# A fused decoder layer: the delta-rule chain of each head squeezed into an earlier part of its projection, and the output projection's operand loaded one unit sooner

## The reference, cut to what matters

```
h = rmsnorm(x, norm1_w[l])
mix, c, sg, sh = token_mixer(h, ...)          # proj = h @ w_in; both head groups; mix @ w_out
x = x + mix
u = jax.nn.relu(rmsnorm(x, norm2_w[l]) @ w_up[l])
x = x + (u * u) @ w_down[l]
```

## Time and profile before

| | before |
|---|---|
| median of 3 runs | 3074.03 us |
| the three runs | 3075.28, 3073.93, 3074.03 us |
| time of the profiled execution | 3074.89 us |
| its span, first to last instruction | 3073.1 us |
| mean granted TensorE clock | 0.986 |
| TensorE busy | 2974.0 us (97%) |
| VectorE busy | 2032.5 us (66%) |
| ScalarE busy | 1202.3 us (39%) |
| share of TensorE in the chain of work that ended last | 86% |

### The profile page before, as it was taken

One profiled execution on the slowest core, in us unless ns is written; L12 is line 12 of the kernel. 1 busy time (PEld: TensorE's weight loads), 2 busy tenths in 40 slices (PEclk: granted clock), 3 DMA queues, 4 the chain that ended last, 5 costly groups with the idle time before them and its releaser, 6 DMA issues.

```text
span 3073.1 us, 52508 instructions
## 1 busy us (share of the span) xinstructions
PE 2974.0 (97%) x22024; PEld 2918.8 (95%) x22024; DVE 2032.5 (66%) x2828; ACT 1202.3 (39%) x1522; POOL 316.9 (10%) x433
## 2 busy tenths in 40 slices
PE   7999999999999999979999999999998999999998
PEld 7999999999999999969999999999998999999998
DVE  5556463637464646545558777777778887878886
ACT  4333333323333333333334444444445444444454
POOL 5010101011101010110210000000000000000021
PEclk9999999999999999989999999999999999999999
DMA  7233563533232334343425444454448666666665
GB/s 211 56 82 64 74 67 53 84 59 83 60 75 61 82 61 82 67 128 104 121 82 153 145 145 156 138 163 136 158 141 276 194 193 196 197 192 192 195 194 192
DMA packets 514107, 392.61 MB, mean 128 GB/s; under 512 B 16752, under 2 KB 483904, under 8 KB 513872
## 3 DMA queue, kind: packets, MB, share of 16 engines
q1 hardware_dynamic: 462272, 268.86, 35.8%
q0 software_dynamic: 22832, 88.39, 7.9%
q10 hardware_dynamic: 28768, 32.00, 3.6%
HBM read 304.87 MB, written 84.33 MB: 127 GB/s over the span
## 4 chain that ended last, share of the span: by engine, by line
PE 86%; DVE 8%; ACT 3%; issue 2%; DMA 1%; POOL 0%; DVEq 0%; ACTq 0%; POOLq 0%
PE main L1267 38%; PE main L918 27%; PE mx L1267 6%; PE mx L1163 2%; PE mx L1062 1%; PE mx L1070 1%; PE mx L994 1%; PE mx L978 1%; DVE w_lo L1803 1%; DVE tmp L1911 1%; PE mx L1021 1%; PE mx L1029 1%; PE mx L1104 1%; PE mx L1170 0%; PE mx L1098 0%
## 5 line engine op out<-in xcount | busy, mean ns | idle before, releaser
L918 PE MATMUL main<-h_hi,w_hi 128*128 128x296 f32 (+1 forms) x2592 | 617.0, 320 | 21.8 <-DVE h_lo L2204 13.8
L1267 PE MATMUL main<-forms_a,w_hi 128*128 128x288 f32 x3072 | 617.9, 296 | 8.5 <-DVE forms_a L2390 4.6
L1267 PE MATMUL main<-forms_b,w_hi 128*128 128x288 f32 x3072 | 613.9, 295 | 7.2 <-DVE forms_b L2390 4.9
L918 PE MATMUL main<-h_lo,w_hi 128*128 128x296 f32 (+1 forms) x2592 | 570.3, 302 | 0.0
L918 PE MATMUL main<-h_hi,w_lo 128*128 128x296 f32 (+1 forms) x2592 | 568.9, 301 | 0.0
L1267 PEld LDWEIGHTS main<-forms_a,w_hi 128*128 128x128 f32 x3072 | 496.9, 189 | 9.6 <-issue 9.4
L1267 PEld LDWEIGHTS main<-forms_b,w_hi 128*128 128x128 f32 x3072 | 492.1, 188 | 8.5 <-issue 5.5
L1267 PE MATMUL main<-forms_a,w_lo 128*128 128x288 f32 x1536 | 456.3, 297 | 0.0
L918 PEld LDWEIGHTS main<-h_hi,w_hi 128*128 128x128 f32 x2592 | 420.5, 193 | 34.5 <-DVE h_lo L2204 15.4
L1267 PE MATMUL main<-forms_b,w_lo 128*128 128x288 f32 x1536 | 452.2, 294 | 0.0
L918 PEld LDWEIGHTS main<-h_lo,w_hi 128*128 128x128 f32 x2592 | 427.9, 192 | 0.0
(11 more groups left out here) (383 smaller groups left out, 3668.7 us busy)
## 6 DMA issues: line engine op xcount, KB each, us to landing
w_raw<-in_w_in SPq DMA_DIRECT2D x130, 512.0 KB, 8.2
w_raw<-in_w_up SPq DMA_DIRECT2D x128, 512.0 KB, 4.1
w_raw<-in_w_down SPq DMA_DIRECT2D x100, 512.0 KB, 4.4
u_forms<-ub POOLq DMA_DIRECT2D x32, 1152.0 KB, 6.7
z<-x_scratch SPq DMA_DIRECT2D x32, 576.0 KB, 7.0
x_scratch<-z POOLq DMA_DIRECT2D x31, 576.0 KB, 3.1
stage<-u_forms ACTq DMA_DIRECT2D x30, 576.0 KB, 4.1
w_raw<-in_w_out SPq DMA_DIRECT2D x32, 512.0 KB, 4.0
```

The source lines that it names most:

```text
L918: ins = mm(out[:, half, :], w[:, ring, k, :], x[:, kx, half * width:half * width + width], start=first and n == 0, stop=last_ and n == 2)
L1267: ins = mm(out, w[:, k, :], x[:, kx, :], start=i in (0, 1, 3) and k == 0 and n == 0, stop=k == KP - 1 and n == 2, skip_group_check=True)
```

## The change

Four tables and a few lines are changed.

1. The GDN chain from `t1` to `st_4` is spread over positions 25 to 57 instead of 25 to 63, so 32 stages take 32 steps rather than 38.
2. `out` of a GDN head is done in the same head, at position 61, and no longer as the stage `gdn_out` at position 2 of the next. `gates`, `conv_in` and `gates_b` of the HGRN2 part move from 3, 6 and 9 to 0, 5 and 8. ScalarE may do the first exponential of `gates` before the last main tile is evacuated.
3. In the last head SyncE issues the loads of k-tiles 0 to 6 of the output projection's operand when the last unit begins (`OUT_U0 - 1`), and no longer when it ends. ScalarE and VectorE split k-tiles 0, 1 and 2 ahead of the last head's GDN `out`.
4. The order of the first k-tiles becomes 0, 1, 2, 3, 7, 4, 5, 6; TensorE does three of them ahead of `turn_v`, and the counts in `FILL_TO` up to `out` are higher. The other splits, and the evacuations and weight splits of the output projection (`EARLY_AT`), are assigned to other stages.

The core of the diff (the two functions `split_hi` and `split_lo` are also moved up, unchanged):

```diff
-K_ORDER = [7] + list(range(7)) + list(range(8, KT))
+K_ORDER = [0, 1, 2, 3, 7, 4, 5, 6] + list(range(8, KT))
...
-SPLITS = {"gdn_out": (0,), "gates": (1,), "gates_b": (2,), "turn_k": (3,), "stw": (4, 5), "diag": (6,), "l1": (7,), "l4": (8,),
-          "l8": (9,), "l16": (10,), "l32": (11,), "l64": (12,), "o": (13, 14), "out": (15,)}
+LATE_SPLITS = {"l2": (8,), "l4": (9,), "l8": (10,), "l16": (11,), "l32": (12,), "l64": (13,), "o": (14,), "out": (15,)}
+SPLITS_HI = {"gates": (3, 4), "gates_b": (5, 6), "turn_v": (7,), **LATE_SPLITS}
+SPLITS_LO = {"gates": (3,), "gates_b": (5,), "turn_v": (6,), "turn_k": (7,), **LATE_SPLITS}
 EARLY = 8
-EARLY_AT = {"l2": 0, "l4": 1, "l16": 2, "l64": 3, "o": 4, "out": 5}
-FILL_TO = {"turn_v": 3, "turn_k": 4, "diag": 7, "l1": 12, "l2": 17, "l4": 22, "l8": 26, "l16": 30, "l32": 34, "l64": 39, "o": 45,
-           "out": 54, "st0": 71}
+EARLY_AT = {"l1": 0, "l2": 1, "l8": 2, "l32": 3, "o": 4, "out": 5}
+FILL_TO = {"gates": 3, "turn_v": 5, "turn_k": 6, "diag": 12, "l1": 16, "l2": 21, "l4": 26, "l8": 30, "l16": 34, "l32": 38, "l64": 43,
+           "o": 49, "out": 58, "st0": 71}
...
-                       + [f"{s}_{c}" for c in range(1, NW) for s in ("ws", "vn", "st")], 25, 63)}
-HG_STAGES = {"gdn_out": 2, "gates": 3, "conv_in": 6, "gates_b": 9, "turn_v": 10, "turn_k": 18, "stw": 20, "diag": 22,
+                       + [f"{s}_{c}" for c in range(1, NW) for s in ("ws", "vn", "st")], 25, 57),
+              "out": 61}
+HG_STAGES = {"gates": 0, "conv_in": 5, "gates_b": 8, "turn_v": 10, "turn_k": 18, "stw": 20, "diag": 22,
...
-            sp.wait_ge(s_unit, OUT_U0)
+            sp.wait_ge(s_unit, OUT_U0 - 1)
             sp.wait_ge(s_gmix, 16 * (HEADS - 1))
-            sp.wait_ge(s_hmix, 16 * (HEADS - 1))
...
+            sp.wait_ge(s_unit, OUT_U0)
+            sp.wait_ge(s_hmix, 16 * (HEADS - 1))
             mix_load(2)
...
-                elif stage == "gates":
+                if stage == "gates":
+                    act.wait_ge(s_evac, h * 8 + 7)
+                    done(A(hf[:, :], hf[:, :], ACT.Exp, scale=-1.0), "exp")
                     act.wait_ge(s_evac, h * 8 + 9)
-                    done(A(hf[:, :], hf[:, :], ACT.Exp, scale=-1.0), "exp")
...
+                                if st == "out" and h == HEADS - 1:
+                                    for n in range(3):
+                                        split_hi(n)
                                 gdn(st, h, first)
...
                     if nxt is None:
-                        split_lo(1)
+                        split_lo(4)
```

More of the change, by code:

```diff
@@ L1129, in hg @@
                 W = lambda steps, name: steps.wait(pe, name, h)
-                if stage == "gdn_out":
-                    gdn("out", h, False)
-                elif stage == "conv_in":
+                if stage == "conv_in":
                     if next_first is not None:
@@ L1547, in hg, with split_hi @@
                     done(A(hl, hl, ACT.Exp, scale=-0.5), "oexp")
+            def split_hi(n):
+                k = K_ORDER[n]
+                if k in (7, 15):
+                    src = go if k == 7 else ho
+                    (gdve if k == 7 else hdve).wait(act, "y", HEADS - 1)
+                    A(h_hi[:, k, 0:NS], src[:, 0:NS], ACT.Copy)
+                    A(h_hi[:, k, NS:TN], src[:, T0:N], ACT.Copy).then_inc(s_k_hi, 1)
+                else:
+                    g = [i for i, (k0, k1) in enumerate(MIX_GROUPS) if k0 <= k < k1][0]
+                    act.wait_ge(s_mixin[g], 32)
+                    A(h_hi[:, k, 0:TN], h_lo[:, k, 0:TN].bitcast(F32), ACT.Copy).then_inc(s_k_hi, 1)
             def head(h, first):
@@ L1565, in _ @@
                 head(h, False)
-            def split_hi(n):
-                k = K_ORDER[n]
-                if k in (7, 15):
-                    src = go if k == 7 else ho
-                    (gdve if k == 7 else hdve).wait(act, "y", HEADS - 1)
-                    A(h_hi[:, k, 0:NS], src[:, 0:NS], ACT.Copy)
-                    A(h_hi[:, k, NS:TN], src[:, T0:N], ACT.Copy).then_inc(s_k_hi, 1)
-                else:
-                    g = [i for i, (k0, k1) in enumerate(MIX_GROUPS) if k0 <= k < k1][0]
-                    act.wait_ge(s_mixin[g], 32)
-                    A(h_hi[:, k, 0:TN], h_lo[:, k, 0:TN].bitcast(F32), ACT.Copy).then_inc(s_k_hi, 1)
             hi(OUT_U0 + 1, (OUT_U0 + 1) % RAW)
@@ L1585, in _ @@
                     hi(u_, u_ % RAW)
-                for n in SPLITS.get(st, ()):
+                for n in SPLITS_HI.get(st, ()):
                     split_hi(n)
@@ L2089, in hg @@
                         dve.wait_ge(s_gmix, h * 16 + 16)
+                    else:
+                        dve.wait_ge(s_k_lo, KT + K_ORDER.index(7) + 1)
                     done(TT(hvx, hvt[:, 0:1, :].to_broadcast([P, SB + 1, P]),
@@ L2149, in save_last, with split_lo @@
                 gdve.done(dve.tensor_copy(last[:, :, n_:n_ + PRE], u[:, :, UW - PRE:UW]), "last")
+            def split_lo(n):
+                k = K_ORDER[n]
+                dve.wait_ge(s_k_hi, KT + n + 1)
+                h = h_hi[:, k, 0:TN].bitcast(F32)
+                if k in (7, 15):
+                    src = go if k == 7 else ho
+                    TT(h_lo[:, k, 0:NS], src[:, 0:NS], h[:, 0:NS], ALU.subtract)
+                    TT(h_lo[:, k, NS:TN], src[:, T0:N], h[:, NS:TN], ALU.subtract).then_inc(s_k_lo, 1)
+                else:
+                    TT(h_lo[:, k, 0:TN], h_lo[:, k, 0:TN].bitcast(F32), h, ALU.subtract).then_inc(s_k_lo, 1)
             def head(h, first):
@@ L2184, in head @@
                             if pos // UK == j - 8:
+                                if st == "out" and h == HEADS - 1:
+                                    for n in range(3):
+                                        split_lo(n)
                                 gdn(st, h, first)
@@ L2230, in _ @@
                 hg(st, HEADS - 1, None)
-                if st != "gates":
-                    for n in SPLITS.get(st, ()):
-                        split_lo(n)
+                for n in SPLITS_LO.get(st, ()):
+                    split_lo(n)
                 if st in EARLY_AT:
```

12 lines of the change are left out of this document (removed).

## The result

The changed kernel takes 3051.11 us (median of four runs, 3046.03 to 3054.05), the kernel before beside it 3073.98 (3073.3 to 3075.28): a ratio of 0.9923 with a 95% interval of 0.9906 to 0.9941, so 22.9 us less. Measured a second time it came to 3049.36 against 3072.59, again 0.9923 (0.9909 to 0.9936). The profiled execution took 3054.05 us, its span is 3052.3 and its mean granted clock 0.990.

A forecast was written before the change was run, and what follows sets the result against it. TensorE, busy for 97% of the span, bounds the kernel, so only its idle and low-clock time can be won. -14.8 + 6.6 - 11.0 = -19.2 us gives a median of 3054.8 us, range 3044 to 3068.

The forecast's parts named there:

- T: The end of the last unit's last k-tile of a head; in the last head, where the projection ends.
- Edit 1, `stw`: HGRN2 part in seven heads: an earlier `out` lets VectorE's copy come in time, so `stw`'s wait goes, -13.8 us.
- Its clock term: Low clock seen after the 4.2 us `stw` wait in one head goes with that wait, -1.0 us.
- Edit 2, `vn_2`: Squeezed GDN chain, eight heads: `vn_2` at unit 6's start waits 1.07 us for VectorE's subtraction, net +6.6 us.
- Rival (a): Squeezed chain: six links cut to one k-tile wait 1.07 us each, 51 us more, 3106; 7%.
- The rule of the Trainium skill: At the eight new waits: an idle array goes to 1.2 GHz, costing +1 to +2 us each; not followed.
- the row: Clock windows of the kernel before: after a 1.5 us `stw` wait the clock stayed at 1.00, so nothing added.
- Edit 3, the end: Where the projection ends: earlier loads and a new order bring `o` to T+61.7, a gain of 11.0 us.
- behind `o` nothing: 0: Behind stage `o`: nothing waited before and the last splits come no later in k-tiles, so 0.
- (b): VectorE isn't ready for `stw`, or new waits bring slow stretches: 3063 us, with both 3070; 12%.
- (c): The end gains little because the operand lands late; nothing gained there gives 3066 us; 11%.
- (d): Better than forecast: no wait at `vn_2` and the end at its bound, -32, 3042 us; 8%.

The follow-up runs named there:

- x1: The kernel before with only the GDN chain squeezed to positions 25 to 57; 3082.45 us, ratio 1.0034.
- x4: The changed kernel with one more k-tile between `ws_2` and `vn_2`, the stages `vn_2` to `vn_4` moved later where room is; 3039.23 us, ratio 0.9891.
- x8: x7 with VectorE's evacuation and weight split at `o` done at `l64` instead; 3034.46 us, ratio 0.9880.
- x2: The changed kernel's heads (squeezed chain, earlier `out` and `gates`) with the old end put back; 3053.01 us, ratio 0.9940.
- x3: The changed kernel with SyncE's operand load put back to the end of the last unit; 3058.24 us, ratio 0.9952.
- x9: The kernel before with GDN's stage `rows` at position 16 in place of 15; 3066.57 us, ratio 0.9978.
- x10: The changed kernel with GDN's stage `rows` at position 16 in place of 15; 3045.51 us, ratio 0.9910.
- x6: The changed kernel with k-tile 3 split ahead of `out` and its low half made ahead of most of `gates` in the last head; 3048.13 us, ratio 0.9924.
- x11: x8 with `rows` at position 16 and the chain from `ws_1` on one k-tile later; 3042.96 us, ratio 0.9906.
- x7: x6 with x4's chain table (`vn_2` two k-tiles behind `ws_2`); median 3039.05 us, ratio 0.9889.

## Why the prediction was right

**The total** was 3054.8 us forecast, 3051.11 measured: -22.9 where I had -19.2. The sign, the range and the mechanisms of the waits held, but two sizes were off in opposite directions: from `rows` to T the change gained 7.7 us more than my terms, at the end 2.0 less. That the total came within 3.7 us is in part luck.

**Edit 1, `stw`** (-13.8 of wait): right. The wait went in all seven heads, the one of 4.2 us too. **Its clock term** (-1.0) was the step that failed most: I looked at the clock behind the `stw` waits, at two places, found one slow, and took it for the whole. The windows of the whole projection show, beside the one that I saw, a slow stretch in each of the seven heads from the second on, right behind `rows`. All of them cost 13.5 us before and 5.2 after. From the second head's `rows` to T the changed kernel gained 13.7 us, and 15.1 when `st_4` and `out` (1.4 us), which now lie ahead of T, are set aside. My terms for that stretch, without the first head's `stw` wait (1.6) and the first `vn_2`, make -14.8 + 1.6 + 5.8 = -7.4. The missing 7.7 us are mostly clock: 13.5 - 5.2 = 8.3, less the 1.0 that I had, is 7.3. That is at the upper end, since the changed kernel's head period, 161.2 or 162.6 us, says 1.4 us for a slow stretch where the windows count 1.7. About 1.1 us more is that `vn_2` cost less than I had.

**Edit 2, `vn_2`** (+6.6): right in place and near in size, 0.91 us instead of 1.07 each: 7.3 us, or +5.3 when the 0.25 us at each `vn_3`, which are too short for the table of waits, are taken off. Rival (a) is refuted: no `p`, `tp` or `st` link waits, in any of the kernels. Alone it cost 10.5 us, not 6.6 (x1), since it lengthened `stw`'s waits and the slow clock too. That the edits hang together is what I had missed: by the medians they gave +10.5 (squeeze alone) and -18.9 (with the earlier `out` and `gates`).

**The rule of the Trainium skill** that I set against the row ("TensorE: Matmul & The Clock Gate", Part 1: an array found idle goes to 1.2 GHz) I had left out of the sum, as the row behind one wait showed nothing. The runs are between the two. Behind the `vn_2` waits themselves no window of the changed kernel's projection is slow, as I had it. But with them 3.4 to 5.2 us of slow clock lie behind `rows`, in six profiles, and without them (x4, x8) none. And x4 gained 10 to 12 us by the removal of 7.3. Why the one goes with the other isn't shown.

**Edit 3, the end** (-11.0). By its steps: loads landed at T-1.9 (forecast T-2.6), the clamp started at T+4.7 (T+4.2), k-tile 3 waited 8.4 us (7.9), `stw` 1.4 (1.0), the levels 0.8, 1.3 and 2.2 (1.0, 1.6, 2.4), and `o` began at T+61.75 (T+61.7). Following one queue with its old durations was good to 0.7 us at each step. What failed is "behind `o` nothing: 0": two waits for the weights' low half, 1.6 and 1.2 us. I had set VectorE's place for them by the counts of k-tiles and not by its clock, on which the evacuation and weight split assigned to `o` and `out` come late. By the traces the end gained 10.4 - 1.4 = 9.0 us. By the medians of x2 and of the changed kernel it is 5.2 (0.9940 to 0.9923), with intervals of 4 us and more on either side of each, so it doesn't contradict the 9.0. x3 shows that the gain hangs on the earlier load, 9.9 us by the trace and 8.9 by the ratios.

**The rivals.** (b) was wrong for `stw` and right in kind for the clock. (c) needed a late operand; it was 0.7 us later than forecast, and x3 shows that a late one would have cost the end all its gain, as I had it. (d) was within reach with one more number in a table: x4 is faster than its 3042, with the end still as forecast. One sum of the chances is wrong: 62, 8, 11 and half of 12 make 0.87, not 0.85.

**What stays open** is why the slow stretches behind `rows` come and go. Three things are shown. Most lie behind `norms` and `rows`, two stages of thin matmuls with one k-tile between them. They don't need the wait there (x9, x10). And they are not set by the program alone: five profiles (the changed kernel twice, x2, x3, x6) have the same order of TensorE's work up to T, and of the seven heads from the second on, numbered 1 to 7, the slow ones are 1, 3 and 6 in the changed kernel's first profile, 3 and 5 in its second, 2, 4 and 7 in x2, 1, 3 and 6 in x3, and 1, 4 and 6 in x6. That is 14 of 35, never two neighbours. Two kernels with a head period of 160.4 us (x4, x8) had none, x10 and x11, at 161.2, had two of seven each, and the kernel before, with 163.5, had one in each of the seven. Here is the same place of the same code in two of these executions, windows in the changed kernel and in x6 (busy us by engine, then granted clock, DMA share, GB/s):

```profile
772.00:774.00 2.00, 2.00 (x12) 1.47 (x12) 1.90 (x3) 0.96 (x2) 0.00 (x0) 1.00 0.36 103
774.00:776.00 2.00, 2.00 (x16) 2.00 (x16) 2.00 (x8) 0.52 (x2) 0.00 (x0) 1.00 0.19 56
```

```profile
768.00:770.00 2.00, 2.00 (x11) 1.60 (x10) 1.90 (x4) 1.36 (x2) 0.00 (x0) 0.80 0.33 96
770.00:772.00 2.00, 2.00 (x9) 2.00 (x9) 2.00 (x7) 0.55 (x1) 0.00 (x0) 0.50 0.12 38
```

The first is at 2.4 GHz throughout, the second falls to 1.2 GHz (0.50), though TensorE is busy in all of its 4 us and its wait at `rows` just before was 0.6 us. The Trainium skill, "TensorE: Matmul & The Clock Gate", Part 1, says that the chip judges the array's activity on a schedule of its own that doesn't start with the kernel; that fits these heads, but no run here moved one program in time alone, so it isn't shown.

## What to carry to other kernels

Add up the granted clock over the whole stretch that a change touches, and not only behind the wait that it removes: here its slow clock fell by 8.3 us as the windows count it, beside 13.8 us of waits that went, and most of it lay elsewhere. A link of a chain that crosses a unit's start, where both elementwise engines have a weight split first, needs one k-tile more than the others (7.3 us of wait, and 10 to 12 us of time when it got one). A long wait at an engine that is paced by another's queue is a place and not a price: x6 halved the largest wait of the kernel and won nothing.

## What the runs showed that I had not expected

One execution of x7 took 7016.18 us, its neighbours 3036.2 to 3039.46. In its profile VectorE's busy time is as ever, but TensorE's is more than twice its usual 2960 us:

```profile
PE 6992.9 (100%) x22024; PEld 6745.0 (96%) x22024; DVE 2046.2 (29%) x2828; ACT 1205.7 (17%) x1522; POOL 301.6 (4%) x433
...
L1269 PE MATMUL main<-forms_a,w_hi 128*128 128x288 f32 x3072 | 1244.7, 516 | 3.3 <-issue 3.3
```

A matmul of 288 columns took 516 ns in the mean there, against 297 in the changed kernel's profile. Here is a piece of 144 of them in the chain that ended last, in x7 and then in the changed kernel:

```profile
3937.22 48.25 PE main L1269 x144
```

```profile
1617.06 19.11 PE main L1268 x144
```

That is one matmul in 0.335 us instead of 0.133. The granted clock can't be read for this execution: its page, alone of all, has no PEclk line, so the 1.00 that the views give for it is no measurement. The lower level alone would hardly do it, since at a granted clock of 0.50 matmuls of the same width followed each other in 0.24 us in the changed kernel (two of them started in 1342.04 to 1342.52 us). It came once among all the executions of this study, and its cause stays open.
